# Two boundaries of a fused transformer kernel by halves of the tokens: residual, split input and the next four weight chunks for tokens 0 to 255, then for 256 to 511

## What is computed

```python
for l in range(DEPTH):                                   # DEPTH = 1
    h = swiglu(rms_norm(x, ffn1_pre[l]), ffn1_w_gu[l], ffn1_w_down[l])
    x = x + 0.5 * rms_norm(h, ffn1_post[l])              # boundary A, first part
    h = token_mixer(rms_norm(x, mix_pre[l]), ...)        # boundary A, second part: times w_in
    x = x + rms_norm(h, mix_post[l])                     # boundary B, first part
    h = swiglu(rms_norm(x, ffn2_pre[l]), ffn2_w_gu[l], ffn2_w_down[l])   # boundary B, second part
    x = x + 0.5 * rms_norm(h, ffn2_post[l])
# rms_norm(x, g) = x * rsqrt(mean(x * x, -1) + 1e-6) * g ; swiglu: (silu(gate) * up) @ w_down
```

## Time and profile before

| | us |
|---|---|
| median of 3 runs | 1931.36 |
| lowest and highest | 1930.75, 1931.91 |
| profiled execution, its own time | 1931.39 |
| its span in the trace | 1929.5 |
| PE busy | 1837.6 (95%) |
| DVE, ACT, POOL busy | 771.9, 434.3, 1267.3 |

### The profile page before, as it was taken

The page is one execution under the profiler, slowest core; times in us unless marked ns, Lnnn a source line. Parts: engine busy times, 40 slices in busy tenths (PEclk is TensorE's granted clock), DMA queues, the critical chain, the costliest instruction groups (busy, mean ns, idle before and its releaser), DMA issues.

```text
span 1929.5 us, 29772 instructions
## 1 busy us (share of the span) xinstructions
PE 1837.6 (95%) x11700; PEld 1459.2 (76%) x11700; DVE 771.9 (40%) x1348; ACT 434.3 (23%) x884; POOL 1267.3 (66%) x621
## 2 busy tenths in 40 slices
PE   8999999988879999999899999998879999999998
PEld 6888888766557888888577786667766878888887
DVE  4333361155564333311323344515745345555301
ACT  3000010034432000000212246644534131112000
POOL 6888888844076888888566643242465867777774
PEclk9999999989989999999899999999999999999999
DMA  4322333221022232233432452140014323233331
GB/s 169 98 93 93 101 94 97 89 87 56 12 87 66 98 98 98 92 91 101 133 132 77 131 181 63 53 164 24 4 52 188 97 87 97 93 94 94 96 95 63
DMA packets 59355, 180.32 MB, mean 93 GB/s; under 512 B 6995, under 2 KB 13907, under 8 KB 58748
## 3 DMA queue, kind: packets, MB, share of 16 engines
q1 hardware_dynamic: 49708, 165.83, 26.6%
q10 hardware_dynamic: 9552, 13.13, 2.0%
HBM read 165.81 MB, written 13.13 MB: 93 GB/s over the span
## 4 chain that ended last, share of the span: by engine, by line
PE 89%; DVE 7%; ACT 2%; issue 2%; DMA 0%; SPq 0%; DVEq 0%; ACTq 0%
PE bank L550 25%; PE bank L551 25%; PE bank L552 25%; PE bank L605 2%; PE bank L904 1%; PE bank L933 1%; PE bank L877 1%; PE bank L839 1%; DVE xT L1790 1%; DVE tmp L1787 1%; PE bank L1092 1%; DVE h_lo L1743 0%; DMA x_tok<-x_dram 0%; DVE X L2243 0%; PE bank L1064 0%
## 5 line engine op out<-in xcount | busy, mean ns | idle before, releaser
L458 POOL TENSOR_TENSOR w_hi<-w_raw,one 128x1024 fp32r<-128x1024 f32 (+1 forms) x279 | 523.3, 1875 | 531.5 <-PE bank L552 522.2
L460 POOL TENSOR_TENSOR w_lo<-w_raw,w_hi 128x1024 fp32r<-128x1024 f32 (+1 forms) x279 | 690.9, 2476 | 21.9
L550 PE MATMUL bank<-h_hi,w_hi 128*128 128x512 f32 x1528 | 618.5, 405 | 20.5 <-DVE h_lo L1743 11.4
L551 PE MATMUL bank<-h_lo,w_hi 128*128 128x512 f32 x1528 | 596.8, 391 | 0.0
L552 PE MATMUL bank<-h_hi,w_lo 128*128 128x512 f32 x1528 | 596.7, 390 | 0.0
L550 PEld LDWEIGHTS bank<-h_hi,w_hi 128*128 128x128 f32 x1528 | 288.2, 189 | 102.5 <-issue 28.5
L551 PEld LDWEIGHTS bank<-h_lo,w_hi 128*128 128x128 f32 x1528 | 288.2, 189 | 67.4 <-issue 10.3
L552 PEld LDWEIGHTS bank<-h_hi,w_lo 128*128 128x128 f32 x1528 | 287.8, 188 | 60.8
L550 PE MATMUL bank<-a_hi,w_hi 128*128 128x512 f32 x528 | 205.5, 389 | 0.0
L552 PE MATMUL bank<-a_hi,w_lo 128*128 128x512 f32 x528 | 205.4, 389 | 0.0
L551 PE MATMUL bank<-a_lo,w_hi 128*128 128x512 f32 x528 | 205.4, 389 | 0.0
(11 more groups left out here) (350 smaller groups left out, 1934.4 us busy)
## 6 DMA issues: line engine op xcount, KB each, us to landing
w_raw<-w_ffn_gu_dram SPq DMA_DIRECT2D x88, 512.0 KB, 3.4
w_raw<-w_conv_up_dram SPq DMA_DIRECT2D x44, 512.0 KB, 3.5
w_raw<-w_ffn_down_dram SPq DMA_DIRECT2D x32, 448.0 KB, 3.3
w_raw<-w_ffn_down_dram SPq DMA_DIRECT2D x16, 512.0 KB, 3.5
w_raw<-w_out_dram SPq DMA_DIRECT2D x16, 512.0 KB, 3.5
w_raw<-w_gates_dram SPq DMA_DIRECT2D x16, 512.0 KB, 3.6
w_raw<-w_rwkv_dram SPq DMA_DIRECT2D x14, 512.0 KB, 3.5
w_raw<-w_conv_down_dram SPq DMA_DIRECT2D x16, 448.0 KB, 3.3
```

The costliest lines, as they stand in the source:

```text
L458: nc.gpsimd.tensor_tensor(w_hi[:, s, 0:width], raw, one[:, 0:1].to_broadcast([P, width]), ALU.mult).then_inc(sem("w_rounded"), 1)
L460: nc.gpsimd.tensor_tensor(w_lo[:, s, 0:width], raw, w_hi[:, s, 0:width].bitcast(F32), ALU.subtract).then_inc(sem("w_split"), 1)
L550: nc.tensor.matmul(dst, hi, rhs_hi[:, k, :], start=start and k == k0, stop=False)
L551: nc.tensor.matmul(dst, hi, rhs_lo[:, k, :], start=False, stop=False)
```

## The change

At boundaries A and B (`HALVED`) everything that lies between the post-norm and the end of chunk 3 is done for tokens 0 to 255 and then again for 256 to 511: `post_norm_halves` on DVE, `norm_ahead_halves` on ACT and `first_four` on PE, all on 128 x 256 tiles. The weight chunks 0 to 3 are all kept until the second half has used them, and `w_used` counts them there. At boundary A the four matmuls for the keys (now lines 719 and 720) come behind chunk 3, not behind chunk 1, and one reload of ACT's function table is gone (`logs()` stays at B alone).

```diff
+HALVED = ("mix", "ffn2")
+TOKENS = (slice(0, S // 2), slice(S // 2, S))
...
+            def first_four(tag, c0, first_bank, sum_bank):
+
+                for half, tokens in enumerate(TOKENS):
+                    def squares(k):
+                        pe.wait_ge(*nth(tag + "_in_sq", KD * half + k + 1))
+                        nc.tensor.matmul(bank[sum_bank][:, tokens], ones, sq[:, k % 2, tokens], start=(k == 0),
+                                         stop=(k == KD - 1)).then_inc(sem(tag + "_in_sq_used"), 1)
+                    for u in range(4):
+                        last = chunk(c0 + u, (c0 + u) % RING, 0, KD, h_hi, h_lo, bank[first_bank + u][:, tokens],
+                                     True, True, None if u else tag + "_h_ready", shift=KD * half,
+                                     also=None if u else squares, tokens=tokens)
+                        if half:
+                            last.then_inc(sem("w_used"), 1)
...
-            mix_in(0)
-            mix_in(1)
+            first_four("mix", FIRST["w_in"], 4, 0)
...
-            mix_in(2)
-            mix_in(3)
...
+            def norm_ahead_halves(tag, gain, x_ready, b):
+
+                for half, tokens in enumerate(TOKENS):
+                    for k in range(KD):
+                        done = KD * half + k
+                        act.wait_ge(*nth(x_ready, done + 1))
+                        nc.scalar.activation(h_hi[:, k, tokens], xT[:, k, tokens], ACT.Copy, scale=param(gain, k))\
+                            .then_inc(sem(tag + "_h_hi"), 1)
+                        if k >= 2:
+                            act.wait_ge(*nth(tag + "_in_sq_used", done - 1))
+                        nc.scalar.activation(sq[:, k % 2, tokens], xT[:, k, tokens], ACT.Square)\
+                            .then_inc(sem(tag + "_in_sq"), 1)
+                inv_rms(tag + "_in", tag + "_in_sq_used", 2 * KD, b=b)
...
+            def post_norm_halves(tag, gain, factor, y, to, next_gain):
...
+                for half, tokens in enumerate(TOKENS):
+                    for k in range(KD):
+                        nc.vector.scalar_tensor_tensor(tmp[:, k % 2, tokens], y[:, k, tokens], param(gain, k),
+                                                       rstd[:, tokens], ALU.mult, ALU.mult)\
+                            .then_inc(sem(tag + "_scaled"), 1)
+                        dve.wait_ge(*nth(tag + "_scaled", KD * half + k + 1))
+                        nc.vector.scalar_tensor_tensor(xT[:, k, tokens], tmp[:, k % 2, tokens], factor,
+                                                       xT[:, k, tokens], ALU.mult, ALU.add)\
+                            .then_inc(sem(tag + "_x_ready"), 1)
+                        if k:
+                            low(half, k - 1)
+                        elif half:
+                            low(0, KD - 1)
+                low(1, KD - 1)
```

More of the change, by code:

```diff
@@ L549, in chunk @@
                     lo = w_lo[:, s, (k - w0) * P:(k - w0 + 1) * P]
-                    nc.tensor.matmul(dst, hi, rhs_hi[:, k, :], start=start and k == k0, stop=False)
-                    nc.tensor.matmul(dst, hi, rhs_lo[:, k, :], start=False, stop=False)
-                    last = nc.tensor.matmul(dst, lo, rhs_hi[:, k, :], start=False, stop=stop and k == k1 - 1)
+                    nc.tensor.matmul(dst, hi, rhs_hi[:, k, tokens], start=start and k == k0, stop=False)
+                    nc.tensor.matmul(dst, hi, rhs_lo[:, k, tokens], start=False, stop=False)
+                    last = nc.tensor.matmul(dst, lo, rhs_hi[:, k, tokens], start=False, stop=stop and k == k1 - 1)
                     if also:
@@ L575, in body @@
                             last.then_inc(sem("w_used"), 1)
-                body(0, True)
+                if tag in HALVED:
+                    first_four(tag, c0, 0, 4)
+                else:
+                    body(0, True)
                 with pe.Fori(1, KF // 2) as i:
@@ L684, in mix_in @@
                 c = FIRST["w_in"] + j
-                chunk(c, c % RING, 0, KD, h_hi, h_lo, bank[4 + j % 4 if j < 6 else 7][:, :], True, True,
-                      "mix_h_ready" if j == 0 else None,
-                      also=(lambda k: sum_square(k, KD, "mix_in_sq", "mix_in_sq_used", 0)) if j == 0 else None)\
+                chunk(c, c % RING, 0, KD, h_hi, h_lo, bank[4 + j % 4 if j < 6 else 7][:, :], True, True)\
                     .then_inc(sem("w_used"), 1)
@@ L1795, in post_norm, with low @@
                     after(KD - 1)
+            def post_norm_halves(tag, gain, factor, y, to, next_gain):
+                dve.wait_ge(*nth(tag + "_post_rstd", 1))
+                dve.wait_ge(*nth(tag + "_y_read", KD))
+                def low(half, k):
+                    tokens = TOKENS[half]
+                    dve.wait_ge(*nth(to + "_h_hi", KD * half + k + 1))
+                    nc.vector.scalar_tensor_tensor(h_lo[:, k, tokens], xT[:, k, tokens], param(next_gain, k),
+                                                   h_hi[:, k, tokens].bitcast(F32), ALU.mult, ALU.subtract)\
+                        .then_inc(sem(to + "_h_ready"), 1)
+                for half, tokens in enumerate(TOKENS):
[12 more added lines that the diff above has]
+                low(1, KD - 1)
             dve.wait_ge(*nth("params_in", 16))
@@ L1831, in _ @@
             sum_out("ffn1")
-            post_norm("ffn1", "ffn1_post", 0.5, yT, after=lambda k: low_part("mix", "mix_pre", k))
+            post_norm_halves("ffn1", "ffn1_post", 0.5, yT, "mix", "mix_pre")
             dve.wait_ge(*nth("mix_in_rstd", 1))
@@ L1976, in _ @@
             add_square(KD - 1)
-            post_norm("wout", "mix_post", 1.0, mixed, after=lambda k: low_part("ffn2", "ffn2_pre", k))
+            post_norm_halves("wout", "mix_post", 1.0, mixed, "ffn2", "ffn2_pre")
             ffn_up("ffn2")
```

18 lines of the change are left out of this document (10 added, 8 removed).

## The result

The changed kernel takes 1942.23 us (median of 5 runs, 1941.11 to 1944.00) beside 1931.91 for the kernel before on the same chip: the medians are 10.3 us apart. The ratio is 1.0046, 95% interval 1.0034 to 1.0058, which is 8.9 us, between 6.6 and 11.2. The profiled execution took 1941.38 us, its span is 1939.6; that is 10.0 us over the profiled execution of before. 1936.0 was forecast, +4.6. The direction and the range held, the size did not.

The account below looks back on a forecast made before the run. PE, busy 95% of the span, was taken to bound the kernel. Block A +2.05, the `rotate_q(0)` wait +0.64 and boundary B +1.9 gave +4.6 us on 1931.4: 1936.0 us, range 1930.5 to 1944.

Parts of the forecast that it names:

- Half k on DVE: At both boundaries, DVE's three instructions for one k at 256 columns take 1.25 us, against 2.05 at full width.
- pitch: PE's time for one float32r matmul of 256 columns: 0.120 us, against 0.227 for 512; forecast case 0.115 to 0.14, 55%.
- first half's chunk 0: Goes by DVE's pace, plus some 0.3 us for the low clock: over 12.2 us into the block.
- ACT's gap: ACT idles some 8 us ahead of the second half's third square while PE runs chunks 1 to 3; DVE idles too.
- `rotate_q(0)`: Behind chunk 3 at A, it waits for the first rotated key, no longer hidden by two chunks: +0.64 us.
- 14.5 + 192 p: Length of boundary A's block in us with the pitch p of its 192 chunk matmuls left open.
- Cheap halves: Rival, 20%: load and matmul cost 0.110 to 0.113 us; sum +1.0 to +2.2, 1932.4 to 1933.6 us.
- loads in line: Rival, 10%: pitch stays near a weight load's 0.19 or at 0.227; blocks +12 to +19 each, 1956 to 1970 us.
- faster: Rival, 5%: DVE's half k about 1.0 us and matmul 0.110; block 32 us, -3.5 at each boundary, 1925 us.
- spreading wait: Rival, 10%: PE-ACT-DVE ring paces the second half's chunk 0, or first half suffers; 2 to 3 us more per boundary, 1940 to 1942.
- Sum. +2.05 + 0.64 + 1.9: Block A 37.5 against 35.45 us, the rotated-key wait, and boundary B: +4.6 us on 1931.4, so 1936.0.
- last condition: Sign that the prediction is wrong: something outside the two boundaries moves.

Follow-up runs that it names:

- e6: The changed kernel again, word for word, on another chip beside the kernel before: 1946.09 us against 1933.12.
- e1: Kernel before plus 209 inert waiting instructions on PE at each boundary, nothing else changed: 1955.13 us against 1933.59, ratio 1.0107.
- e10: Kernel before plus 64 inert waiting instructions on PE at boundary A: 1939.24 us against 1932.24, ratio 1.0037.
- e11: Kernel before plus 64 inert waiting instructions on PE at each boundary: 1938.12 us, ratio 1.0030.
- e2: Changed kernel plus 47 inert waiting instructions on PE at each boundary, nearly restoring the code's place: 1937.84 us against 1933.59, ratio 1.0022.
- e9: Kernel before at full width, chunks 0 and 1 side by side for each k, key matmuls behind chunk 2: 1931.46 us against 1932.24, ratio 0.9994.
- e12: e9 plus four inert float32 matmuls of 256 columns on PE ahead of each block: 1933.42 us against the kernel before's 1933.57, ratio 1.0001.
- e5: Kernel before plus 81 inert matmuls of 64 x 64 on PE at boundary A: 1950.55 us against 1933.12, ratio 1.0079.

## Why the prediction was right and wrong

**Right, step by step, at the boundaries.** Half k on DVE 1.25; first matmul after 2.33 forecast, 2.34 measured; pitch 0.120, 0.120; first half's chunk 0 to 12.2, 11.9; ACT's gap 8, 7.92; `rotate_q(0)` 0.64, 0.56; weights no cost: PE waits for no split. Block A 37.5 forecast, 37.0 measured. The half microsecond lies in both chunks 0: the first half's is over 0.3 sooner, and the second half's, put at 8.0, takes 7.8 (from 408.4 to 416.2). B +1.9, measured +1.7; its terms as written, 37.3 + 0.1 - 35.4, make 2.0. (The forecast's low end, 1933.5 at a pitch of 0.115, is 1934.1 by its own 14.5 + 192 p. Nothing hangs on either.) Together +4.6, against +3.8 in the changed kernel's trace and +4.7 in e6's. The halves lose for the reason given: PE is nearly always busy at a boundary, and 192 short matmuls cost more than 96 long ones.

**The rivals.** Cheap halves and loads in line fell with the pitch of 0.120 (the 0.109 that the prediction names beside its own is 11 ns short, as at 512 columns), faster with the half k. The spreading wait fell too, though its 1940 to 1942 comes within 0.3 us of the measured time: the second half's chunk 0 took less than forecast, not 2 to 3 us more. The time alone would have named the wrong cause. That 1942.2 lies in the range of 1930.5 to 1944 is luck: the range was wide for a pitch of 0.14 and for the spreading wait, and neither came true.

**Wrong: the step from two boundaries to the whole.** "Sum. +2.05 + 0.64 + 1.9" lets everything behind keep its length. The last condition, "or if something outside the two boundaries moves", is the one that failed: 4.8 of the 10 us arose in the RWKV stage. What the runs showed in its place is that 450 more instructions on PE move the ends of its code blocks against the stage, and its issue waits rise from 3 to 10 us, the stage by some 5 (134.7 to 139.5 in the mean of the table). This is shown by inert code alone (e1, e10, e11), taken back by filling up (e2), and independent of when the stage starts: e1's starts 21 us later than that of before and e10's 3 us, with the same waits. The page of before didn't show it: the chain's "issue", 2% of the span, is some 39 us, of which PE's issue waits are 3.2. I had costed PE's new instructions by their run time and not by their place.

**The accounts.** +1.55 + 0.56 + 1.67 at the boundaries, +4.8 in the stage and +1.2 behind it are 9.8 of the 10.0 us between the profiled executions. The rest is the sum of steps of up to 1 us either way, most beside stretches of half clock that fall elsewhere.

**Open.** Why PE goes on only 1.24 to 1.54 us behind the packet's end, and why the threshold lies between a shift of 32 and one of 64. That a block's end costs nothing where PE waits anyway is argued from the rows, not tried: no run moved a single end. Nor was it settled what makes the stretches of half clock between 1040 and 1200 us come in some executions.

## What to carry to other kernels

Where an engine runs dense small instructions, the length of its code ahead of them is part of the cost of any edit: compare its issue waits in untouched stages before you explain a difference, and test with inert instructions whether an edit's gain or loss is only its place. Price a boundary by what the busiest engine idles there, not by how long the others stand still: 8 us of stall on ACT and DVE were worth 1.6. An order that leaves nothing between a norm and the first user of its result pays for the norm's tail.

## What the runs showed of the hardware

- Code blocks: packets of 16 KB on q8 for some 256 instructions of PE; issue waits of 0.2 to 1.6 us each, which in the first traces of before and after end 1.24 to 1.54 us behind a packet's end; 0.5 to 3.9 against 8.5 to 10.2 us in one stage by the place of the code.
- An instruction on PE that only waits for two semaphores long reached took 0.07 us (105 in 7.08); 47 at a boundary cost nothing that the trace of e2 shows, 209 at each of the two cost 14.6 us together in e1.
- A square sum of 256 columns in float32 took 0.43 us where a float32r matmul of the same width took 0.120, and counts as two matmuls and two loads in PE's code.
- Four float32 matmuls of 256 columns in an idle gap of PE brought the half clock at the start of boundary A from 10.2 us (e9) to 3.4 (e12). With 81 of 64 x 64 in the same gap, which ran for 17.3 us without a pause, the granted clock stayed at half for 20.5 us (e5).
